# A three-stage transformer kernel: raw compression weights as moving operand, rotary products on a split operand, output linears reordered

## The reference, cut to what matters

```python
def compress_blocks(t, pos_emb, w1, b1, w2, b2):
    idx = np.arange(nc)[:, None] * CMP_STRIDE + np.arange(CMP_BLOCK)[None, :]
    blocks = t[:, :, idx, :] + pos_emb                   # 31 blocks of 32 tokens, 2 heads
    flat = blocks.reshape(B, G, nc, CMP_BLOCK * dh)      # 2048 values each
    return jax.nn.gelu(flat @ w1 + b1) @ w2 + b2         # w1: 2048 x 256

def hybrid_layer(x, ...):
    proj = rmsnorm(x, norm_mix) @ w_in
    ...
    q_n = partial_rope(to_heads(q_b, NSA_HEADS), pos)
    kc = partial_rope(compress_blocks(kc, ...), cmp_end_positions(T))
    vc = compress_blocks(vc, ...)
    ks, kw = partial_rope(ks, pos), partial_rope(kw, pos)
    ...
    mixed = jax.nn.sigmoid(gate_a) * y_a + jax.nn.sigmoid(gate_b) * y_b
    x = x + mixed @ w_out
    h = rmsnorm(x, norm_mlp)
    return x + jnp.square(jax.nn.relu(h @ w_up)) @ w_down
```

## Time and profile before

| | |
|---|---|
| median of 3 runs | 2231.97 us (2231.52 to 2234.8) |
| the profiled execution | 2231.35 us |
| its span, first to last instruction | 2229.6 us |
| TensorE products busy | 2198.7 us, 99% |
| TensorE weight loads busy | 1751.1 us, 79% |
| VectorE busy | 1162.8 us, 52% |
| ScalarE busy | 607.4 us, 27% |
| GpSimd busy | 1500.5 us, 67% |
| HBM read | 191.82 MB |

### The profile page before, as it was taken

How to read it: one execution, slowest core, us unless ns; L and a number is a source line. 1 busy time by engine, 2 the same in 40 slices (tenths; PEclk the granted TensorE clock), 3 DMA queues, 4 the chain that set the end, 5 groups by cost and what they waited for, 6 DMA issues and landing times.

```text
span 2229.6 us, 29899 instructions
## 1 busy us (share of the span) xinstructions
PE 2198.7 (99%) x11018; PEld 1751.1 (79%) x11019; DVE 1162.8 (52%) x1934; ACT 607.4 (27%) x1435; POOL 1500.5 (67%) x679
## 2 busy tenths in 40 slices
PE   9999999999999999999999999999999999999998
PEld 6876788888887867778788888878677787888886
DVE  8769667773353285557640243552665477411422
ACT  5248222221021165531220121111455412200210
POOL 7650687778875614448887888756334488888884
PEclk9999999999999999999999999999999999999999
DMA  5320233333323301112333333233111123333332
GB/s 193 111 76 1 76 95 95 97 102 97 111 95 114 114 29 58 51 54 95 95 103 96 95 96 103 86 113 114 58 39 58 58 84 93 99 101 95 95 98 73
DMA packets 54921, 195.79 MB, mean 88 GB/s; under 512 B 7312, under 2 KB 7312, under 8 KB 54544
## 3 DMA queue, kind: packets, MB, share of 16 engines
q1 hardware_dynamic: 52496, 187.85, 26.5%
q10 hardware_dynamic: 2304, 6.22, 0.8%
HBM read 191.82 MB, written 2.10 MB: 87 GB/s over the span
## 4 chain that ended last, share of the span: by engine, by line
PE 90%; DVE 6%; issue 2%; ACT 1%; DMA 0%; POOL 0%; SPq 0%; DVEq 0%
PE bank L491 25%; PE bank L493 25%; PE bank L492 25%; PE bank L606 3%; PE bank L616 3%; PE bank L653 1%; DVE t L1292 1%; PE bank L507 1%; PE bank L577 1%; PE bank L635 1%; DVE prow L1405 1%; PE bank L656 1%; DVE bank L1394 1%; PE bank L568 1%; ACT prow L1016 1%
## 5 line engine op out<-in xcount | busy, mean ns | idle before, releaser
L436 POOL TENSOR_TENSOR w_hi<-w_raw,zero 128x1024 fp32r<-128x1024 f32 x336 | 657.4, 1957 | 677.0 <-PE bank L493 663.4
L439 POOL TENSOR_TENSOR w_lo<-w_raw,w_hi 128x1024 fp32r<-128x1024 f32 x336 | 844.6, 2514 | 26.5
L491 PE MATMUL bank<-hn_hi,w_hi 128*128 128x512 f32 x1632 | 648.9, 398 | 6.4 <-POOL w_lo L439 3.2
L493 PE MATMUL bank<-hn_hi,w_lo 128*128 128x512 f32 x1632 | 636.2, 390 | 0.0
L492 PE MATMUL bank<-hn_lo,w_hi 128*128 128x512 f32 x1632 | 635.9, 390 | 0.0
L491 PEld LDWEIGHTS bank<-hn_hi,w_hi 128*128 128x128 f32 x1632 | 306.6, 188 | 76.5 <-issue 8.3
L492 PEld LDWEIGHTS bank<-hn_lo,w_hi 128*128 128x128 f32 x1632 | 306.8, 188 | 64.2 <-issue 3.4
L493 PEld LDWEIGHTS bank<-hn_hi,w_lo 128*128 128x128 f32 x1632 | 306.5, 188 | 64.5
L491 PE MATMUL bank<-hid_hi,w_hi 128*128 128x512 f32 x688 | 267.9, 389 | 0.0
L493 PE MATMUL bank<-hid_hi,w_lo 128*128 128x512 f32 x688 | 267.8, 389 | 0.0
L492 PE MATMUL bank<-hid_lo,w_hi 128*128 128x512 f32 x688 | 267.8, 389 | 0.0
(11 more groups left out here) (294 smaller groups left out, 2666.3 us busy)
## 6 DMA issues: line engine op xcount, KB each, us to landing
w_raw<-wstream SPq DMA_DIRECT2D x352, 512.0 KB, 3.5
x<-xT SPq DMA_DIRECT2D x4, 512.0 KB, 7.7
out<-yout ACTq DMA_DIRECT2D x8, 256.0 KB, 2.2
mem_x<-memT SPq DMA_DIRECT2D x1, 1024.0 KB, 12.7
lnc<-lncount ACTq DMA_DIRECT2D x1, 1024.0 KB, 5.6
cs<-trig ACTq DMA_DIRECT2D x2, 512.0 KB, 4.3
par<-params ACTq DMA_DIRECT2D x1, 696.0 KB, 5.6
bc<-bconst ACTq DMA_DIRECT2D x1, 664.0 KB, 6.8
```

The costliest lines, as they stand in the source:

```text
L436: nc.gpsimd.tensor_tensor(w_hi[:, slot, :], w_raw[:, slot, :], zeros, ALU.add).then_inc(w_rounded, 1)
L439: nc.gpsimd.tensor_tensor(w_lo[:, slot, :], w_raw[:, slot, :], w_hi[:, slot, :].bitcast(f32), ALU.subtract).then_inc(w_split, 1)
L491: nc.tensor.matmul(ps[bank][:, 0:cols_], wh, a_h, start=c == 0, stop=False)
L493: mm = nc.tensor.matmul(ps[bank][:, 0:cols_], wl, a_h, start=False, stop=c == chunks - 1)
```

## The change

1. **The join's operands are exchanged.** `linear_w1` takes `cmp_g` as the stationary operand (128 x 64, the last two columns zero) and 256 columns of `w_raw` as the moving one. Even chunks go to PSUM partitions 0 to 63, odd ones to 64 to 127, all of them into 256 columns of bank 7. A group is now 4 products in place of 8; both tiles of keys (or of values) add into the same columns. The weight stream is laid out to fit; its bytes and blocks stay the same.
2. **A fold follows.** ScalarE copies the 128 x 256 sums to `w1sum`; `fold_w1` multiplies each half of 128 columns with a constant of ones that adds the upper to the lower partitions and turns the result at once: 2 fp32 products of 62 columns into bank 4. It is issued in the middle (after chunk 4) of linears 15 and 25. ScalarE waits for it and then applies bias and gelu, two activations.
3. **Rotary products of the later layers are split.** ScalarE's copy goes to `rope_hi` (rounded), VectorE makes `rope_lo` from the bank and `rope_hi`, in its place of the job itself, and `rotate_split` issues two fp32r products with a rounded copy of `rot`. The first block keeps `rotate`.
4. **The step behind a `w1` tile's place moves.** The rotation or the transposes of the job before are issued in the middle of the next linear.
5. **The output linears are led by the first.** Instead of turns chunk by chunk: six chunks of the first, two of the second, the last two of the first, the last six of the second.

```diff
             def linear_w1(t, half):
 
-                kind, n, block_, _, bank, _, _ = tiles[t]
-                if half == 0:
-                    pe.wait_ge(*took(last_on_bank[bank]))
-                    last_on_bank[bank] = t
-                for c in range(8 * half, 8 * half + 8):
-                    b_, j = block_ + c // 8 * 3, c % 8
-                    if j == 0:
-                        pe.wait_ge(w_split, b_ + 1)
-                    mm = nc.tensor.matmul(ps[bank][:, 0:2 * NCMP], w_raw[:, b_ % RING, j * P:(j + 1) * P],
-                                          cmp_g[:, n // 2, c * 2 * NCMP:(c + 1) * 2 * NCMP], start=c == 0, stop=c == 15)
-                    if j == 7:
-                        mm.then_inc(blocks_done, 1)
+                _, n, block_, _, bank, _, _ = tiles[t]
+                kv, b_, q = n // 2, block_ + 3 * half, 2 * (n % 2) + half
+                pe.wait_ge(w_split, b_ + 1)
+                for c in range(4 * q, 4 * q + 4):
+                    rows, j = slice(64 * (c % 2), 64 * (c % 2) + 64), c % 4
+                    mm = nc.tensor.matmul(ps[bank][rows, kv * 256:(kv + 1) * 256], cmp_g[:, kv, c, :],
+                                          w_raw[:, b_ % RING, j * 256:(j + 1) * 256], start=c < 2, stop=c >= 14)
+                mm.then_inc(blocks_done, 1)
+
+            def fold_w1(l, kv):
+
+                pe.wait_ge(w1_kept, 2 * l + kv + 1)
+                for f in range(2):
+                    a_ = P + (2 * kv + f) * 2 * NCMP
+                    mm = nc.tensor.matmul(ps[4][:, a_:a_ + 2 * NCMP], w1sum[:, f * P:(f + 1) * P], fold,
+                                          start=True, stop=True)
+                mm.then_inc(w1_folded, 1)
...
+            def rotate_split(n, slot):
+                pe.wait_ge(roped, n - len(ROPE))
+                nc.tensor.matmul(ps[5][:, :], rot_r[:, :], rope_hi[:, slot, :], start=True, stop=False)
+                nc.tensor.matmul(ps[5][:, :], rot_r[:, :], rope_lo[:, slot, :], start=False, stop=True).then_inc(rotated, 1)
...
+                    if kind in ("qr", "kr"):
+                        pe.wait_ge(rot_rounded, l + 1)
+                        pe.wait_ge(rope_split, 6 * l + idx_of_rope(t) + 1)
+                        rotate_split(roped_n, roped_n % 2)
...
+                    elif i < len(jobs) - 1 and i > 2 and tiles[jobs[i - 1]][0] == "w1":
+                        linear(jobs[i], hn_hi, hn_lo, S, DC, part=(0, 4))
+                        finish(i - 2)
+                        linear(jobs[i], hn_hi, hn_lo, S, DC, part=(4, DC))
+                    elif i in (15, 25):
+                        linear(jobs[i], hn_hi, hn_lo, S, DC, part=(0, 4))
+                        if i == 15:
+                            pe.wait_ge(fg_parts, l + 1)
+                        fold_w1(l, i // 25)
+                        linear(jobs[i], hn_hi, hn_lo, S, DC, part=(4, DC))
...
-                    if 0 <= i - 1 < len(jobs):
...
+                    if 0 <= i - 1 < len(jobs) and not (i < len(jobs) and tiles[jobs[i]][0] == "w1"):
+                        finish(i - 1)
...
-                linear_pair(ph["out"][0], ph["out"][1], mx_hi, mx_lo, (mix_split, DC * l))
+                first, second = ph["out"][0:2]
+                linear(first, mx_hi, mx_lo, S, DC, (mix_split, DC * l), part=(0, 6))
+                linear(second, mx_hi, mx_lo, S, DC, part=(0, 2))
+                linear(first, mx_hi, mx_lo, S, DC, (mix_split, DC * l), part=(6, DC))
+                linear(second, mx_hi, mx_lo, S, DC, part=(2, DC))
```

On ScalarE:

```diff
-                    if i >= 2 and tiles[jobs[i - 2]][0] == "w1":
+                    if i >= 2 and tiles[jobs[i - 2]][0] == "w1" and tiles[jobs[i - 2]][1] % 2:
                         t = jobs[i - 2]
-                        idx = tiles[t][1]
+                        kv = tiles[t][1] // 2
                         act.wait_ge(blocks_done, filled(t))
-                        A(hidc[:, idx // 2, idx % 2, :], ps[tiles[t][4]][:, 0:2 * NCMP], ACT.Gelu_apprx_tanh,
-                          bias=pcol(f"b1_{'kv'[idx // 2]}{l}", idx % 2)).then_inc(w1_took, 1)
+                        A(w1sum[:, :], ps[7][:, kv * 256:(kv + 1) * 256], ACT.Copy).then_inc(w1_kept, 1)
+                        act.wait_ge(w1_folded, 2 * l + kv + 1)
+                        for f in range(2):
+                            a_ = P + (2 * kv + f) * 2 * NCMP
+                            A(hidc[:, kv, f, :], ps[4][:, a_:a_ + 2 * NCMP], ACT.Gelu_apprx_tanh,
+                              bias=pcol(f"b1_{'kv'[kv]}{l}", f)).then_inc(w1_took, 1)
```

On VectorE, once per layer and for each rotary job:

```diff
+                V.memset(cmp_g[:, :, :, 2 * NCMP:], 0.0)
+                V.tensor_copy(rot_r[:, :], rot).then_inc(rot_rounded, 1)
...
+                    if i < len(jobs) and tiles[jobs[i]][0] in ("qr", "kr"):
+                        kind, idx, _, _, bank = tiles[jobs[i]][:5]
+                        n = 6 * l + idx_of_rope(jobs[i])
+                        dve.wait_ge(rope_in, n + 1)
+                        V.scalar_tensor_tensor(out=rope_lo[:, n % 2, :], in0=ps[bank][:, :],
+                                               scalar=-0.125 if kind == "qr" else 1.0,
+                                               in1=rope_hi[:, n % 2, :].bitcast(f32), op0=ALU.mult,
+                                               op1=ALU.subtract).then_inc(rope_split, 1)
```

More of the change, by code:

```diff
@@ L172, in build @@
         Q += (NPAR * 4 + 31) // 32 * 32
-        fc = at("fc", [5 * P + S + 32], f32, Q)
-        Q += (5 * P + S + 32) * 4
+        fc = at("fc", [5 * P + S + 96], f32, Q)
+        Q += (5 * P + S + 96) * 4
         bc = at("bc", [5 * P + 4 * 248 + 8 * P], bf16, Q)
@@ L186, in build @@
         valid0 = fc[:, 5 * P + S:5 * P + S + NCMP]
+        fold = fc[:, 5 * P + S + 32:5 * P + S + 32 + 2 * NCMP]
         identb, causal = bc[:, 0:P], bc[:, P:5 * P]
@@ L274, in build @@
                 c = o + TURNS + 6 * n
-                ph["in"].append(tile("w1", n, c, 4))
+                ph["in"].append(tile("w1", n, c, 4, 7))
                 ph["in"] += [tile(k, i, c + (1, 2, 4, 5)[m], 1) for m, (k, i) in enumerate(four)]
@@ L555, in norm_spread, with linear_pair @@
                 mm.then_inc(norm_row, 1)
-            def linear_pair(ta, tb, hi, lo, ready, n=None):
+            def linear_pair(ta, tb, ready, n=None):
                 for c in range(DC):
-                    linear(ta, hi, lo, S, DC, ready, part=(c, c + 1))
-                    linear(tb, hi, lo, S, DC, part=(c, c + 1))
+                    linear(ta, hn_hi, hn_lo, S, DC, ready, part=(c, c + 1))
+                    linear(tb, hn_hi, hn_lo, S, DC, part=(c, c + 1))
                     if n is not None and c == 3:
@@ L855, in _, with finish @@
                 on_bank = {tiles[t][4]: t for t in jobs}
-                spare = (norm_rt, 4 + 2 * l)
+                spare = (w1_kept, 2 * l + 2)
                 first_free = [spare if b == 7 else took(on_bank[b]) for b in ((2, 7, 0, 1) if l == 0 else (0, 1, 2, 7))]
+                def finish(m):
+                    nonlocal roped_n, v_done
+                    t = jobs[m]
+                    kind = tiles[t][0]
+                    if kind in ("qr", "kr"):
+                        pe.wait_ge(rot_rounded, l + 1)
+                        pe.wait_ge(rope_split, 6 * l + idx_of_rope(t) + 1)
+                        rotate_split(roped_n, roped_n % 2)
+                        roped_n += 1
+                    if kind == "v":
+                        pe.wait_ge(*took(t))
+                        pe.wait_ge(v_kept, v_done)
+                        turn_tile(sq[:, v_done % 2, :], 6, TT).then_inc(v_turned, 1)
+                        v_done += 1
                 for i in range(len(jobs) + 2):
@@ L861, in _ @@
                     if i < len(jobs) and tiles[jobs[i]][0] == "w1":
+                        if tiles[jobs[i]][1] == 0:
+                            pe.wait_ge(norm_rt, 4 + 2 * l)
                         if tiles[jobs[i]][1] % 2 == 0:
@@ L1892, in _constants @@
     valid0[:, :NCMP] = end[None, :] <= p[:, None]
+    n = np.arange(64)
+    both = ((p[:, None] % 64 == n[None, :]) & (n[None, :] < 2 * NCMP)).astype(f)
     fconst = np.concatenate([np.eye(P, dtype=f), rot, headmean, np.full((P, P), 1 / D, f),
-                             np.full((P, P), 1 / CONV_W, f), tri, valid0], axis=1)
+                             np.full((P, P), 1 / CONV_W, f), tri, valid0, both], axis=1)
     causal = np.concatenate([np.zeros((P, 3 * P), f), np.where(p[None, :] > p[:, None], f(BIG), f(0))], axis=1)
```

33 lines of the change are left out of this document (13 added, 20 removed).

## The result

The changed kernel takes 2213.3 us (median of 4 runs, 2212.25 to 2214.36) against 2231.78 (4 runs): ratio 0.9914, 95% interval 0.9897 to 0.9931. That is 18.5 us less where 13.9 were forecast; the forecast's range began at 2213.5. The profiled executions are 2231.35 and 2212.25 us, their spans 2229.6 and 2210.5: 19.1 us apart.

The account below looks back on a forecast made before the run. TensorE, busy for 99% of the span, was taken as the bound. Terms -10.1 - 1.5 - 4.4 + 2.0 + 0.9 - 0.8 = -13.9 us from the median 2231.97 gave 2218.1 us, range 2213.5 to 2222.5.

Parts of the forecast that it names:

- Part 1: Compression's first layer: weights as moving operand, overlapping PSUM halves, 1.10 instead of 1.73 us per group, 16 groups; -10.1 us.
- part 2: Second weight tile: the stall on the bank VectorE still adds from disappears, 0.74 us in both layers; -1.5 us.
- part 3: Later layers' rotary products: two split products replace one fp32 product in 12 rotations, VectorE's splits covered; -4.4 us.
- part 4: Fold: four new fp32 visits in the middle of linears, 0.5 us each; +2.0 us.
- part 5: Turns of v: four transposes moved inside linears pay two mode changes instead of one; +0.9 us.
- Part 6: First output linears: the new order removes the second tile's bank wait on VectorE, once, in layer 0; -0.8 us.
- no price: Streamed blocks, DMA and GpSimd's splits: unchanged work, GpSimd's next split still early in the input stage; put at nothing.
- Chunk 7: First output tile's last mix chunk: wanted at 1034.0, VectorE finishes at 1033.8, just fits; otherwise 0.1 to 0.3 us return.
- Late waits: Joined tile's copy, fold, activations and second compression layer miss their cover, about 1 us per place; 2222 us, chance 0.10.
- No overlap: Compression weight groups: the two halves run one after the other, 1.96 us per group; 2231.9 us, chance 0.06.
- Late rests: Rotary products wait for VectorE's split, which ends about 7 us after its linear; 2239 us, chance 0.04.

Follow-up runs that it names:

- the run with one half: Changed kernel with all sixteen join products of a tile pair sent to PSUM partitions 0 to 63, the fold contracting 64 partitions; 2227.15 us.
- plain order: Changed kernel with the first output tile computed whole and then the second; 2215.96 us.
- same lead behind the norms: Changed kernel with the 6, 2, 2, 6 chunk order also for the first two linears behind each norm; 2214.0 us.
- pair in turns with squares in PSUM: Changed kernel with the first two output linears again alternating by chunk, and the squares of the norm behind them in PSUM; 2214.01 us.

## Why the prediction was wrong, by its own steps

**Direction and stage** were right: the gain lies in TensorE's own stream, the input stages.

Every term of the sum came out near its size; what failed is a term that was put at nothing. **Part 1** (-10.1), **part 2** (-1.5), **part 3** (-4.4), **part 4** (+2.0) and **part 5** (+0.9) sum to -13.1 us; the two input stages measured -13.7. Group: 1.10 forecast; 1.01 plus 0.09 of entry measured. Rotations: -4.4, the run without them +4.9. Fold visit: 0.5, measured 0.46. The last two make up the 0.6 us between sum and measurement; parts 2 and 5 were not measured alone. The Trainium skill's page "TensorEngine Tiling (Array Packing)" says, in its section Tiling Modes, that changing the tiling mode drains the engine, and the trace after agrees, with 0.09 us on entering the group. With no price for entry and exit the term would have been 16 x (1.73 - 0.92) = 13.0, about 3 us too large. The transfer from the attention's row to the join was right, and the run with one half shows that it was the overlap.

**Part 6** is the step that failed. Its first half, the bank wait of 0.8 us, measured 0.86. But "no price: GpSimd splits the same blocks ... so the next split is still early" looked at the input stage's load alone, and TensorE's waits for GpSimd in the list of waits were never asked what set them. Two of them, 1.4 us each, stood at the pair behind this very norm. The order of the output linears moved the release of a ring slot by about 4 us, and GpSimd, which before had worked at 5.02 us a block against TensorE's 5.44 and was still late at the pair, stayed ahead; the two waits went. A term put at nothing was 3.8 us. With the norm's product, whose wait shrank by 0.33, and the slower first steps behind a wait, 1.84 and 1.94 us came in addition: 3.8 us of the 5.2 by which the two spans (19.1 apart) miss the forecast. The rest is 0.6 in the input stages, 0.54 in layer 1's attention, and 0.27 before the first edit, where TensorE's program is the same and the runs scatter by 0.8. The 0.54 arises in the first 8 us of that stage: VectorE's two scalings of `prow` took 1.45 us before and 1.01 after, beside one split of GpSimd that ended 1.17 and 0.74 us after they began. That fits the same hold-up between the two engines, but no run isolates it.

**Chunk 7** "just fits" was right: no wait in its place, and 1.0 us of wait when it is asked for 1.4 us earlier.

**Rivals.** Late waits did not occur: TensorE waits for nothing in the input stage after. No overlap did not occur either; the one-half run shows what it would have cost, +13.9 us. Late rests did not occur: no rotary product waited for VectorE. The range was too narrow on its lower side because it held no case in which a wait outside the edited stages goes away. The median lies only 0.2 us below it, less than the runs scatter, so whether it was hit is chance; the 3.8 us in two stages forecast at 0 are not.

## What to carry to other kernels

When a step moves, write down when it gives back each buffer and follow that to the engine that refills it; the wait that this removes or makes can lie 40 us later, in a stage that no edit touches. An engine that is 67% busy is not early because of that: a refill chain that runs at 5.0 us against 5.4 gains 2.9 us over seven blocks and can't make up a start that is 4.3 us later. And products with 64 output rows can be issued in turns to the two halves of PSUM's partitions: a group of four took 1.01 us in place of 1.87, with entry and exit (0.09 and about 0.10 us here) paid once per group.

## What the runs showed of the hardware that was not expected

The granted clock of TensorE fell to 0.50, the lower of its two levels (1.2 in place of 2.4 GHz), for about 3 us at a time, in the middle of several profiles. Two of the cases stand above, behind the waits of 1.97 us in the run without the moved steps. Three other profiles (plain order, same lead behind the norms, pair in turns with squares in PSUM) have layer 1's attention at 246.86 to 246.88 us instead of 245.22, and each of them has such a stretch 13 us into that stage. The same three microseconds in the run with the lead behind the norms and in the kernel after:

```profile
core 0: us, PE busy (x) PEld busy (x) DVE busy (x) ACT busy (x) POOL busy (x), PEclk, DMA share, GB/s
1572.00:1575.00 3.00, 3.00 (x12) 1.50 (x9) 2.27 (x9) 1.20 (x5) 0.00 (x0) 0.50 0.03 5
```

```profile
1572.00:1575.00 3.00, 3.00 (x28) 1.79 (x26) 2.88 (x13) 2.13 (x8) 0.00 (x0) 1.00 0.02 5
```

12 product records instead of 28 start in it; each such stretch costs 1.6 us. Just before it TensorE had waited 1.13 and 0.17 us in the one and 1.14 and 0.17 in the other, so the same instructions with the same waits went either way.

The run with the order alone shows two such stretches in layer 0's attention, from 789 to 792 and from 800 to 802 us; that stage took 250.70 us where it takes 245.95 in the other profiles. It began with VectorE: its two scalings of `prow` took 3.49 us in place of 1.45, while two of GpSimd's operations ran beside them without a pause (783.68 to 787.96), and TensorE stood for 0.32, 1.49 and 0.27 us. By then it was 1.9 us behind the kernel before, and the remaining 2.8 came with the two slow stretches. It was no part of the edit, which comes later in the program; layer 1's same stage took 245.85. Such episodes are as large as this change's missing term, so single spans of this kernel should be compared by stage, and the granted clock of a stage read first.
